# A hybrid decoder trunk on one core: the order of the head's chain, unread fp32 products, and final-norm turns with diag(final_g)

## The reference, cut to what matters

```python
def rmsnorm(x, g):
    y = x * lax.rsqrt(jnp.mean(x * x, axis=-1, keepdims=True) + EPS)
    return y * g

mod = (silu(c) @ w_ada + b_ada)          # sh1, sc1, g1, sh2, sc2, g2
hn = rmsnorm(x, norm1_g) * (1.0 + sc1) + sh1
proj = hn @ w_in                         # then convolutions, RG-LRU, w_out
x = x + g1 * mix
...
x = x + g2 * ((gelu(uc) * v) @ ffn_w_down)
...
y = rmsnorm(x, final_g)                  # after the last layer
```

## Time and profile before

| | us |
|---|---|
| median of 3 runs | 1337.21 |
| lowest and highest | 1336.83, 1337.5 |
| the profiled execution, its time | 1338.02 |
| its span, first to last instruction | 1336.4 |
| TensorE busy | 1308.4 (98%) |
| VectorE, ScalarE busy | 711.2 (53%), 489.1 (37%) |
| mean granted clock of TensorE | 0.995 |

### The profile page before, as it was taken

The page is one execution under the profiler, slowest core; times in us unless marked ns, Lnnn a source line. Parts: engine busy times, 40 slices in busy tenths (PEclk is TensorE's granted clock), DMA queues, the critical chain, the costliest instruction groups (busy, mean ns, idle before and its releaser), DMA issues.

```text
span 1336.4 us, 23646 instructions
## 1 busy us (share of the span) xinstructions
PE 1308.4 (98%) x9715; PEld 1247.3 (93%) x9715; DVE 711.2 (53%) x1259; ACT 489.1 (37%) x647; POOL 47.6 (4%) x94
## 2 busy tenths in 40 slices
PE   5999999999999999999999999999999999999998
PEld 4788888899999999999999888999999999999997
DVE  4463863675444543554487186367544454354545
ACT  5424753453233222232344376245322222123231
POOL 0300000000000000000010000000000000000001
PEclk9999999999999999999999999999999999999999
DMA  9654655522222222222243565411222221222202
GB/s 300 211 173 175 220 190 189 190 72 72 97 93 78 94 71 87 85 72 94 66 142 99 185 212 174 150 64 64 80 84 94 91 94 65 94 73 85 94 32 97
DMA packets 115837, 157.10 MB, mean 118 GB/s; under 512 B 3543, under 2 KB 108984, under 8 KB 110645
## 3 DMA queue, kind: packets, MB, share of 16 engines
q1 hardware_dynamic: 108413, 112.55, 25.6%
q0 software_dynamic: 7168, 43.47, 9.5%
q10 hardware_dynamic: 184, 0.06, 0.0%
HBM read 153.08 MB, written 2.99 MB: 117 GB/s over the span
## 4 chain that ended last, share of the span: by engine, by line
PE 92%; DVE 4%; DMA 2%; ACT 1%; issue 1%; DVEq 0%; SPq 0%; POOLq 0%; ACTq 0%
PE ps L381 25%; PE ps L383 24%; PE ps L382 24%; PE ps L400 4%; PE ps L401 4%; PE ps L402 4%; PE ps L447 3%; DMA ada_w<-in_w_ada 2%; DVE w_lo L1018 1%; PE ps L529 1%; PE ps L624 1%; PE ps L458 1%; DVE norm_lo L1028 0%; DVE work L1086 0%; ACT w_hi L719 0%
## 5 line engine op out<-in xcount | busy, mean ns | idle before, releaser
L381 PE MATMUL ps<-norm_hi,w_hi 128*128 128x288 f32 x1792 | 533.1, 297 | 0.0
L382 PE MATMUL ps<-norm_lo,w_hi 128*128 128x288 f32 x1792 | 528.6, 295 | 0.0
L383 PE MATMUL ps<-norm_hi,w_lo 128*128 128x288 f32 x1792 | 526.8, 294 | 0.0
L381 PEld LDWEIGHTS ps<-norm_hi,w_hi 128*128 128x128 f32 x1792 | 335.8, 187 | 16.8 <-issue 15.9
L383 PEld LDWEIGHTS ps<-norm_hi,w_lo 128*128 128x128 f32 x1792 | 337.5, 188 | 0.0
L382 PEld LDWEIGHTS ps<-norm_lo,w_hi 128*128 128x128 f32 x1792 | 336.5, 188 | 0.0
L1018 DVE TENSOR_TENSOR w_lo<-w_raw,w_hi 128x2048 fp32r<-128x2048 f32 x91 | 208.4, 2290 | 87.6 <-ACT w_hi L719 87.5
L719 ACT ACTIVATE w_hi<-w_raw 128x2048 fp32r<-128x2048 f32 x91 | 173.8, 1910 | 156.7 <-PE ps L383 152.4
L381 PE MATMUL ps<-mid_hi,w_hi 128*128 128x288 f32 x704 | 209.3, 297 | 0.0
L382 PE MATMUL ps<-mid_lo,w_hi 128*128 128x288 f32 x704 | 207.7, 295 | 0.0
L383 PE MATMUL ps<-mid_hi,w_lo 128*128 128x288 f32 x704 | 207.0, 294 | 0.0
(11 more groups left out here) (212 smaller groups left out, 1376.3 us busy)
## 6 DMA issues: line engine op xcount, KB each, us to landing
w_raw<-in_ffn_w_up SPq DMA_DIRECT2D x44, 1024.0 KB, 5.0
ada_w<-in_w_ada POOLq DMA_DIRECT2D x40, 1024.0 KB, 5.2
w_raw<-in_w_in SPq DMA_DIRECT2D x20, 1024.0 KB, 5.5
w_raw<-in_ffn_w_down SPq DMA_DIRECT2D x16, 1024.0 KB, 5.2
ada_first<-in_w_ada SPq DMA_DIRECT2D x8, 1024.0 KB, 10.3
w_raw<-in_w_out SPq DMA_DIRECT2D x8, 1024.0 KB, 5.2
w_raw<-in_ffn_w_down SPq DMA_DIRECT2D x8, 768.0 KB, 4.4
work<-in_x_prompt SPq DMA_DIRECT2D x4, 512.0 KB, 6.9
```

The source lines that it names most:

```text
L381: T.matmul(out, WH[:, r, k, c:c + P], xh[:, k, h, :], start=start, stop=False)
L382: T.matmul(out, WH[:, r, k, c:c + P], xl[:, k, h, :], start=False, stop=False)
L383: last = T.matmul(out, WL[:, r, k, c:c + P], xh[:, k, h, :], start=False, stop=stop)
```

## The change

At the head VectorE makes all six copies of X. The first half's reciprocal and diagonal come after three tiles. TensorE turns the first vectors after the third tile of x, spreads the first half after the fifth, waits for ScalarE's copy of the spread (which frees the bank), transposes the sixth, and spreads the second half. After the first turn it makes three products of a 1/1024 matrix with chunks of X into a bank that nobody reads. The main matmuls then wait for less: chunks 0 and 1 of the first half for two output tiles, then for the third tile after `lo_half`, then the second product and the second half. VectorE and ScalarE have the order to match; the spread's copy and the scaled rows have other places in the work buffer.

At the end `final_g` goes on a diagonal (`FGD`, made by VectorE) and the transposes become plain fp32 matmuls with it, so that the row product only needs the token's factor. ScalarE makes rows 0, 1, 2, 4 and half of 5, VectorE row 3 and the other half of 5. The last square isn't added to the sum; instead the means take two accumulating matmuls for each token tile. Semaphores count each row by itself.

```diff
 # tensor, head
-            pe.wait_ge(x_moved, 5)
-            for h in range(2):
-                norm_spread(1, h)
+            for j in range(3):
+                x_tile(j)
             pe.wait_ge(c_ready, 1)
             pe.wait_ge(v_first, 16 * NFIRST)
             n = VT[0][1]
             T.transpose(PS[:, B_MISC, 0:n], VROW[0:n, vrow(0, 0), :], IDN[0:n, 0:n]).then_inc(v_cols, 1)
+            for j in (3, 4):
+                x_tile(j)
+            pe.wait_ge(x_moved, 3)
+            norm_spread(1, 0)
+            pe.wait_ge(rs_copied, 1)
+            x_tile(5)
+            pe.wait_ge(x_moved, 6)
+            norm_spread(1, 1)
             first_product(0)
             pe.wait_ge(v_ready, 1)
             first_turn(0)
-            first_three(0)
+            keep_busy(3)
+            pe.wait_ge(norm_ready, 1)
+            pe.wait_ge(head_lo, 1)
+            for k in range(2):
+                first_part(k, 0, (0, 1))
+            pe.wait_ge(lo_half, 1)
+            for k in range(2):
+                first_part(k, 0, (2,))
             first_product(1)
-            first_three(1, 1)
+            pe.wait_ge(norm_ready, 2)
+            first_part(0, 1, (0, 1, 2))
+            first_turn(1)
+            first_part(1, 1, (0, 1, 2))
...
+            def keep_busy(n):
+                for k in range(n):
+                    T.matmul(PS[:, B_ADA, 0:HALF], AVG[:], X[:, k, 0, :], start=True, stop=True)
...
+            def first_part(k, h, tiles):
+                for i in tiles:
+                    half_chunk(i, i, k, h, NH, NL)
 # scalar, head
+            for j in range(5):
+                token_squares(j)
+            spread_row(0)
+            token_squares(5)
             act.wait_ge(v_cols, 1)
             A(VEC[:, 0, 0:108], PS[:, B_MISC, 0:108], ACT.Copy).then_inc(v_ready, 1)
...
+            spread_row(1)
             first_row(0)
 # vector, head
+            for j in range(3):
+                move_tile(j)
             dve.wait_ge(v_cols, 1)
             rstd(1, 0)
+            for j in range(3, 6):
+                move_tile(j)
             rstd(1, 1)
...
+            dve.wait_ge(x_moved, 6)
+            dve.wait_ge(rs_copied, 1)
+            scaled(1, 0, rs0)
             dve.wait_ge(v_ready, 1)
+            first_modulation(0)
+            sample_part(1, MOD_SH1, 0)
+            head_low(0, 0)
             dve.wait_ge(rs_copied, 2)
+            scaled(1, 1, rs0)
+            norm_low(1, 0)
+            sample_part(1, MOD_SH1, 1)
+            head_low(1, 0)
+            scaled(1, 2, rs0)
+            norm_low(1, 1)
+            head_low(0, 1)
+            head_low(1, 1)
 # tensor, end
-                    last = T.transpose(PS[0:w, Y_BANK[j] + k // 4, (k % 4) * P:(k % 4 + 1) * P], X[:, k, h, t0:t0 + w], IDN[:])
+                    last = T.matmul(PS[0:w, Y_BANK[j] + k // 4, (k % 4) * P:(k % 4 + 1) * P], X[:, k, h, t0:t0 + w], FGD[:, k, :],
+                                    start=True, stop=True)
...
-            norm_stats(L * 2 + 1, 1)
+            pe.wait_ge(last_square, 1)
+            for t0, w, c in half_tiles(1):
+                out = stat_bank(L * 2 + 1, 1)[0:w, c:c + 1]
+                T.matmul(out, acc_of(1)[:, t0:t0 + w], AVG[:, 0:1], start=True, stop=False)
+                last = T.matmul(out, halves(SQ[1])[:, 1, t0:t0 + w], AVG[:, 0:1], start=False, stop=True)
+            last.then_inc(stat_done, 1)
 # scalar, end
+            square(L * 2 - 1, 8)
+            square(L * 2 - 1, 9)
+            y_scaled(0, slice(0, 2))
+            y_scaled(1, slice(0, 2))
+            square(L * 2 - 1, 10)
+            y_scaled(2, slice(0, 2))
+            act.wait_ge(x_ready, L * 24)
+            A(halves(SQ[1])[:, 1], X[:, KX - 1, 1], ACT.Square).then_inc(last_square, 1)
             std(L * 2 + 1, 1)
+            y_scaled(4, slice(0, 2))
+            y_scaled(5, slice(1, 2))
 # vector, end
             dve.wait_ge(fg_in, 16)
+            V.tensor_tensor(FGD, FGB.rearrange("p (k n) -> p k n", k=KX),
+                            IDN[:].rearrange("p (u n) -> p u n", u=1).broadcast_to([P, KX, P]), ALU.mult).then_inc(fg_ready, 1)
             sum_square(L * 2 - 1, 8)
             half_residual(*end, 9)
-            y_row(0)
             sum_square(L * 2 - 1, 9)
-            y_row(1)
             half_residual(*end, 10)
-            y_row(2)
             sum_square(L * 2 - 1, 10)
             half_residual(*end, 11)
-            sum_square(L * 2 - 1, 11)
             rstd(L * 2 + 1, 1)
-            for j in (3, 4, 5):
-                y_row(j)
+            y_scaled(3, slice(0, 2))
+            y_scaled(5, slice(0, 1))
```

More of the change, by code:

```diff
@@ L173, in turned, with scaled_rows @@
             return PS[:, 2 * (i % 3):2 * (i % 3) + 2, :].rearrange("p b (q n) -> p (b q) n", n=P)
+        def scaled_rows(m):
+            return T1_HEAD if m == 1 else T1
         def stat_bank(m, h):
@@ L211, in hybrid_trunk_kernel @@
         x_cols, lam_e = sem("x_cols"), sem("lam_e")
-        x_copied, x_moved = sem("x_copied"), sem("x_moved")
-        fg_in, y_cols, y_rows, y_out = sem("fg_in"), sem("y_cols"), sem("y_rows"), sem("y_out")
+        x_moved = sem("x_moved")
+        fg_in, fg_ready, y_cols, y_out = sem("fg_in"), sem("fg_ready"), sem("y_cols"), sem("y_out")
+        y_row = [sem(f"y_row{j}") for j in range(6)]
+        last_square, rst_ready = sem("last_square"), sem("rst_ready")
         first_full = [sem(f"first_full{b}") for b in range(4)]
@@ L522, in _, with x_tile @@
             T.transpose(PS[:, B_MISC, 0:72], VROW[0:72, 14, :], IDN[0:72, 0:72]).then_inc(c_cols, 1)
[L523 to L524 removed]
+            def x_tile(j):
+                i, h, t0, w = token_tiles()[X_ORDER[j]]
                 pe.wait_ge(x_in[i], 16)
                 if j >= 3:
[L527 removed]
+                    pe.wait_ge(x_moved, j - 2)
                 for k in range(KX):
@@ L762, in norm_round @@
                 n, (p, h) = m * 8 - 8 + j, pair_and_half(m, j)
-                f, t = (halves(r[j % 2]) for r in (HID, T1))
+                f, t = (halves(r[j % 2]) for r in (HID, scaled_rows(m)))
                 act.wait_ge(*((norm_f if m == 1 else t1_ready), n + 1))
@@ L800, in _, with token_squares @@
             act.wait_ge(dve_step, 2)
[L801 to L805, removed]
+            def token_squares(j):
+                i, h, t0, w = token_tiles()[X_ORDER[j]]
                 act.wait_ge(x_in[i], 16)
@@ L988, in _, with y_scaled @@
             std(L * 2 + 1, 0)
-            for i in range(8, 12):
-                square(L * 2 - 1, i)
+            def y_scaled(j, banks):
+                i, h, t0, w = token_tiles()[Y_ORDER[j]]
+                act.wait_ge(y_cols, j + 1)
+                act.wait_ge(rst_ready, h + 1)
+                A(YROW[i][0:w].rearrange("p (b n) -> p b n", b=2)[:, banks], PS[0:w, Y_BANK[j]:Y_BANK[j] + 2, :][:, banks],
+                  ACT.Copy, scale=RST[0:w, 3 * h + t0 // P:3 * h + t0 // P + 1]).then_inc(y_row[j], 1)
+            square(L * 2 - 1, 8)
[6 more added lines that the diff above has]
+            A(halves(SQ[1])[:, 1], X[:, KX - 1, 1], ACT.Square).then_inc(last_square, 1)
             std(L * 2 + 1, 1)
+            y_scaled(4, slice(0, 2))
+            y_scaled(5, slice(1, 2))
         @block.vector
@@ L1066, in rstd @@
                 dve.wait_ge(std_ready, m * 2 + (h - 1))
-                step(V.reciprocal(RST[:, c:c + 3], STD[:, c:c + 3]))
+                ins = V.reciprocal(RST[:, c:c + 3], STD[:, c:c + 3])
+                if m == 2 * L + 1:
+                    ins.then_inc(rst_ready, 1)
+                    dve.wait_ge(rst_ready, h + 1)
+                else:
+                    step(ins)
                 if m == 1:
@@ L1235, in first_modulation @@
                 step(V.tensor_tensor(gain, gain, g, ALU.mult))
+            rs0 = [halves(RS0)[:, h] for h in range(2)]
+            dve.wait_ge(x_moved, 6)
+            dve.wait_ge(rs_copied, 1)
+            scaled(1, 0, rs0)
             dve.wait_ge(v_ready, 1)
+            first_modulation(0)
+            sample_part(1, MOD_SH1, 0)
+            head_low(0, 0)
             dve.wait_ge(rs_copied, 2)
-            rs0 = [halves(RS0)[:, h] for h in range(2)]
-            scaled(1, 0, rs0)
-            for b in range(4):
+            scaled(1, 1, rs0)
[6 more added lines that the diff above has]
+            head_low(1, 1)
+            for b in range(1, 4):
                 first_modulation(b)
```

55 lines of the change are left out of this document (21 added, 34 removed).

## The result

The changed kernel takes 1341.48 us in the median of 14 runs (1338.77 to 1344.83), against 1336.96 of the kernel before in the same rounds: a ratio of 1.0032, 95% interval 1.0024 to 1.0040. It is slower by 3.2 to 5.3 us. I had said 1339.3 in a range from 1335.4 to 1342.2; the time is in the range and the direction is the forecast's, but the size is twice what I had taken for the likeliest. It lies beyond the 0.2% that I had called no change and given 0.55; a larger loss had 0.35.

The account below looks back on a forecast made before the run. TensorE, busy 98% of the span, was taken to bound the kernel. Head -2.15 and end +4.25 us sum to +2.1 on the median 1337.21: 1339.3 us, range 1335.4 to 1342.2.

Parts of the forecast that it names:

- The end: Last part of the kernel: dearer turns 2.7, later means 1.65, output 0.1 earlier; together +4.25 us, bounds +3.2 and +6.9.
- T to the means' result: From the last main matmul's end to the means' result: 4.25 us instead of 2.6, so +1.65 us.
- the output held by bytes: Kernel's end: the last output is bound by its traffic, not the row products; rows on two engines bring -0.1 us.
- The three tiles in front of T: 24 turns between main matmuls, before the last one ends, hidden by nothing: 0.22 instead of 0.109 us each, +2.7 us.
- The rival of turns at a transpose's price: At the end, each turn takes 0.109 us and the end costs nothing: 1335.1, or 1333.7 with clock held; chance 0.10.
- the one of four times it: At the end, each turn takes 0.435 us, four times a transpose: 1347.5 us in all; chance 0.03.
- The head: Before the main work: first main matmul 0.8 us earlier, clock's gain 1.35 us; together -2.15 us.
- the rival with the late first product: At the head, the clock rises only after the first product ends at 25.8: head +0.5, total 1342.0 us; chance 0.17.
- The first product starts at 22.3 instead of 21.55: At the head, waits for ScalarE's spread copy and the sixth square behind it delay the first modulation product to 22.3.
- 5.85 us: At the head, time from the first product's end to the first main matmul, which was 7.43 us before.
- The clock's return: At the head, unread products shorten TensorE's standstill; half of the 2.7 us lost to low clock comes back, 1.35 us.
- A shift passes through: Behind the head, the order and engines stay the same, so an earlier first main matmul reaches the end in full.

Follow-up runs that it names:

- end alone: Only the end's part of the change, head as in the kernel before; 1341.32 us, ratio 1.0031 to the kernel before.
- one line alone: The kernel before with the end's transposes made fp32 matmuls with the identity, nothing else changed; 1341.19 us, ratio 1.0030.
- after: The kernel with the whole change, head and end, against the kernel before; 1341.48 us, ratio 1.0032.
- head alone: Only the head's part of the change, with three unread products, end as in the kernel before; 1337.53 us, ratio 1.0001.
- the spreads together: The head's part, end as before, with the sixth tile's transposes put back ahead of both spreads; 1336.12 us, ratio 0.9989 to the kernel before.
- head alone again: Second series of the kernel with only the head's part changed, three unread products kept; 1338.07 us, ratio 1.0003 to the kernel before.

## Why the prediction was right at the end and wrong at the head

**The end, predicted +4.25.** Right: end alone is +4.1. A turn was put at 0.22 us and is 1.78 / 8 = 0.223; 14 turns at 3.1, measured 3.12; T to the means' result at 4.25, measured 4.03; the output held by bytes, -0.1, measured 0. The three tiles in front of T were put at 2.7 and cost 3.0 in the traces. That VectorE's sum falls away helps nobody, as said. The rival of turns at a transpose's price and the one of four times it are both out: one line alone costs 4.0 us, and its records say twice.

**The head, predicted -2.15.** Wrong: 0 (twice, each within 1.3 us). That is the whole of the sum's error, 4.3 instead of 2.1. The time stayed in the range because the range was wide enough for a head that gives nothing. It lies near the 1342.0 of the rival with the late first product, but not by its mechanism: in after the product ends at 21.34, not behind 25.8. Four steps of the working have to be told apart.

- "The first product starts at 22.3 instead of 21.55" rested on transposes at the slow pace, 1.85 us a tile. That was the one trace I had. In the four other traces with the old head the last 16 transposes take 1.70 us, 0.11 each, and TensorE waits 1.6 us and then 0.8 to 1.7 for the diagonals ahead of the two spreads. The first product starts at 19.74 to 20.51 there, and at 18.07 to 20.80 in the four with the whole new head, 1.1 us earlier in the mean of all and not 0.75 later. The waits that I named (copy 0.50, sixth square 1.76) are there, but the old head has waits of the same size.
- "5.85 us" from the product's end to the first main matmul is right at the upper clock: in after 27.23 - 21.34 = 5.89. In head alone it is 6.69, as the turn runs at the low clock (1.84). This is the price I gave to the late-product rival; it came in traces where the clock had fallen at 17 to 19, a fall that I hadn't seen coming. I had also called 1062 and 592 ns the ratio of the two levels; it is 1.8, and the product as a whole is the better measure, 3.64 us low and 1.92 high.
- The clock's return, half of 2.7 us for the products: the medians show none of it. In after they end at 24.75, the clock falls at 27.7 all the same, and the main work runs low until 31.1 and again from 38 to 41.3. The 5.4 us of low clock that I started from were one trace's too: in the five traces with the old head the clock comes back 2.8 to 6.0 us after the first main matmul. Leaving the products out gained 1.3 us here (1.0001 to 0.9988) and, with the spreads together, 1.2 (0.9989 to 0.9980). Why they cost is not shown: TensorE waited there anyway in the traces compared.
- "A shift passes through" is the step that took the gain away. In the traces the head is 2.0 us earlier at chunk 2, near the 2.15 predicted, but by luck: it is made of an earlier first product and a shorter way from there, without the clock's share. Then 2.3 us of added waits for w_ada stand between chunk 2 and the end. Earlier still, in after, the product at 38.02 waited 1.25 us for the third modulation block (the DMA engines moved 347 to 352 GB/s in nearly every two microseconds from 12 to 46 us); that wait is there in three of the nine traces with the new head. Which loads collide, and why the new head waits longer for w_ada even where it is not earlier, stays open.

## What to carry to other kernels

An fp32 matmul by a diagonal is no free scaling on a TensorE that is busy all the time: each turn is two records and 0.223 us where a transpose is one and 0.109, and 24 of the 38 turns lie where nothing hides them. Moving rows to a second engine was worth nothing here, where the last three transfers form one block of traffic that starts behind the first row (6.8 us from root to end either way). A gain at the head of a kernel should be followed to the first wait for a transfer behind it, and a term that rests on one trace's clock should be widened to what a second trace of the same kernel shows. Here two traces of the kernel before differ by 1.5 us at the first product and 1.9 at chunk 2, as much as the gain that was looked for.

## What the runs showed of the hardware

- A 128-column fp32 matmul with 128 weight columns takes 0.11 us for each of two records at 2.4 GHz (28 in 3.12), a transpose 0.109 in one. The Trainium skill (TensorE: Matmul & The Clock Gate, Terms) calls transpose mode "4× faster for FP32"; here, at this size, it is two times against a plain fp32 matmul.
- At the start of a trace the windows show 1.00 as the granted clock, whatever the pace: in the first trace of before transposes run 0.19 us apart under that number. The pace has to be read from the distance of starts.
- TensorE can reach its upper clock on transposes alone: in after 24 of them start at 6.45 and the 16 from 11.07 on take 0.12 each. The Trainium skill (the same page, Part 4) says that the full clock doesn't engage for transposes; this trace does not agree.
- The clock falls and rises up to three times ahead of 42 us, at different places in different executions of one kernel: under the first main work it is low from 27.1 to 37.4 in the first trace of before and from 27.2 to 34.0 in the second, and head alone again gave mean granted clocks from 0.992 to 0.997 and times from 1335.38 to 1340.20.
